# First two quarters of the first round's w2 in finished buffers, with 4 KB of scratch for dynamic transfers

## The reference

```python
def hier_moe(h, w_group, b_group, w_expert, b_expert, w1, w3, w2):
    ...                      # the router picks 2 of 64 experts for each token
    def expert_block(args):
        xb, e = args
        return (jax.nn.silu(xb @ w1[e]) * (xb @ w3[e])) @ w2[e]
    y_disp = lax.map(expert_block, (x_disp.reshape(n_blocks, MOE_BLOCK, d), blk_expert)).reshape(rows, d)
    y = jax.ops.segment_sum(y_disp[dest] * w_sorted[:, None].astype(y_disp.dtype), tok_sorted, num_segments=t)
    return y.reshape(b, s, d)
```

## Time and profile before

| | us |
|---|---|
| median of 3 runs | 1448.33 |
| lowest and highest | 1446.87, 1449.07 |
| the profiled execution's own time | 1447.13 |
| its span | 1445.3 |

### The profile page before, as it was taken

One profiled execution on the slowest core, in us unless ns is written; L12 is line 12 of the kernel. 1 busy time (PEld: TensorE's weight loads), 2 busy tenths in 40 slices (PEclk: granted clock), 3 DMA queues, 4 the chain that ended last, 5 costly groups with the idle time before them and its releaser, 6 DMA issues.

```text
span 1445.3 us, 14719 instructions
## 1 busy us (share of the span) xinstructions
PE 1028.2 (71%) x5933; PEld 532.5 (37%) x5933; DVE 457.4 (32%) x932; ACT 166.1 (11%) x409; POOL 59.1 (4%) x94
## 2 busy tenths in 40 slices
PE   4999999999999986466465664665645646566366
PEld 1867688655455442122121221212212212122121
DVE  1255477443467361121120211212112112021121
ACT  1132222012233210000000000000000000000000
POOL 4000210011020000000000000000000000000000
PEclk9999999999999999788887887878868878788688
DMA  9946656656626579999999999999999999999996
GB/s 352 370 169 239 240 219 233 230 95 204 225 85 243 205 296 428 428 428 428 427 429 428 429 428 428 429 429 428 429 429 429 429 429 428 429 429 427 428 426 260
DMA packets 78638, 503.75 MB, mean 349 GB/s; under 512 B 5318, under 2 KB 10718, under 8 KB 54020
## 3 DMA queue, kind: packets, MB, share of 16 engines
q1 hardware_dynamic: 75872, 496.22, 83.8%
q0 software_dynamic: 2656, 6.93, 2.1%
q10 hardware_dynamic: 68, 0.02, 0.0%
HBM read 501.54 MB, written 1.61 MB: 348 GB/s over the span
## 4 chain that ended last, share of the span: by engine, by line
PE 50%; DMA 41%; DVE 4%; SPq 3%; issue 1%; ACT 0%; DVEq 0%
DMA flex<-in_w_dram 23%; DMA arena<-in_w_dram 14%; PE ps L542 11%; PE ps L531 10%; PE ps L1011 9%; PE ps L1036 7%; PE ps L986 3%; PE ps L1054 2%; DMA ring<-in_w_in_dram 2%; DMA ring<-in_w_ada_dram 2%; SPq L387 1%; PE ps L768 1%; SPq L393 1%; DVE arena L2009 1%; PE ps L663 1%
## 5 line engine op out<-in xcount | busy, mean ns | idle before, releaser
L1011 PE MATMUL ps<-ring,arena 128*32 128x512 f32 x1024 | 258.8, 663 | 97.2 <-DMA arena<-in_w_dram 94.6
L1011 PE MATMUL ps<-arena 128*32 128x512 f32 x768 | 258.3, 662 | 96.7 <-DMA flex<-in_w_dram 93.9
L1036 PE MATMUL ps<-arena 128*32 128x512 f32 x384 | 146.6, 733 | 67.0 <-DMA flex<-in_w_dram 66.3
L1036 PE MATMUL ps<-ring,arena 128*32 128x512 f32 x512 | 146.7, 736 | 65.4 <-DMA arena<-in_w_dram 64.6
L542 PE MATMUL ps<-ring,flex 128*128 128x512 f32 (+1 forms) x368 | 155.7, 579 | 0.4 <-ACT flex L1104 0.4
L531 PE MATMUL ps<-flex,ring 128*128 128x256 f32 x640 | 147.7, 388 | 3.1 <-DMA ring<-in_w_in_dram 2.4
L1011 PEld LDWEIGHTS ps<-ring,arena 128*32 128x32 f32 x1024 | 66.5, 121 | 176.1 <-issue 174.7
L531 PEld LDWEIGHTS ps<-flex,ring 128*128 128x128 f32 x640 | 122.1, 194 | 22.1 <-issue 3.0
L1011 PE MATMUL ps<-flex,arena 128*32 128x512 f32 x256 | 129.6, 665 | 0.0
L1011 PEld LDWEIGHTS ps<-arena 128*32 128x32 f32 x768 | 60.2, 120 | 176.4 <-issue 173.6
L2009 DVE TENSOR_TENSOR arena<-ps,grow 128x1024 f32<-128x1024 f32 x15 | 18.4, 1224 | 264.3 <-PE ps L1036 264.3
(11 more groups left out here) (385 smaller groups left out, 1022.8 us busy)
## 6 DMA issues: line engine op xcount, KB each, us to landing
ring<-in_w_dram SPq DMA_DIRECT2D x92, 2048.0 KB, 19.8
arena<-in_w_dram SPq DMA_DIRECT2D x69, 2048.0 KB, 24.0
flex<-in_w_dram SPq DMA_DIRECT2D x23, 2048.0 KB, 28.6
ring<-in_w_in_dram SPq DMA_DIRECT2D x17, 2048.0 KB, 10.2
ring<-in_w_ada_dram SPq DMA_DIRECT2D x14, 2048.0 KB, 8.3
ring<-in_w_ada_dram SPq DMA_DIRECT2D x8, 1024.0 KB, 17.9
ring<-in_w_out_dram SPq DMA_DIRECT2D x4, 2048.0 KB, 9.7
ring<-in_w_dram SPq DMA_DIRECT2D x16, 512.0 KB, 13.2
```

What stands on the lines that cost most here:

```text
L1011: mm = pe.matmul(ps[32 * e:32 * e + 32, g, :], xe3[:, c, 32 * e:32 * e + 32], mslot(slots[e])[:, c * W5:(c + 1) * W5], start=c == 0, stop= ...
L1036: mm = pe.matmul(ps[32 * e:32 * e + 32, 2 + n, :], actT3[:, j, 32 * e:32 * e + 32], mslot(slots[e])[:, o:o + W5], start=j == 0, stop=j == ...
```

## The change

- **Pieces ahead.** Quarters 0 and 1 of round 0's w2 are cut in 16 pieces of 256 KB (quarter j, expert e, half n), each with a home outside the eight places: parts of `grow`, `arena`, `hoT`, `cst`, `wr`, `wrs`, `mod2p` whose contents are no longer needed, and six pieces in a new tensor `spare` (`ahead_of`). SP issues 12 of them behind the first load of w3, after waits for `st_wr` and `cv_w2`, and 4 behind the last load of w3, after waits for `x_ok` and `gr_sum`.
- **Quarters 2 and 3** of that w2 go into the first two quarters of places 0 to 3, at `first_free` 1 and 2.
- **w1 of round 1** is loaded in quarters too, at `second_free` 1 to 3 (raised at c = 1, 3, 5 of round 0's w3 product) and `mring_free` 2, where before it was four loads of 2 MB at `mring_free` 2. PE waits for the first three quarters on `third_in`.
- **Memory.** `hoT` is now declared with all 128 partitions (33 were used, and still are by its first reader). `spare` takes 12 KB of each partition, and the scratch that GpSimd's dynamic DMAs use shrinks from 16 KB to 4 KB of each partition.

```diff
+AHEAD = 2
...
-        hoT = sb("hoT", BM, parts=33)
+        hoT_all = sb("hoT", BM)
+        hoT = hoT_all[0:33, :]
+        spare = sb("spare", 6 * W5)
...
+        def ahead_of(j, e, n):
+            homes = [grow[:, 0:W5], grow[:, W5:D], ar(3584, W5), hoT_all[:, 0:W5], cst[:, C_S1:C_S1 + W5], wr[:, 0:W5]]
+            homes += [spare[:, k * W5:(k + 1) * W5] for k in range(6)]
+            homes += [grow[:, D:D + W5], grow[:, D + W5:2 * D], wrs[:, 0:W5], mod2p[:]]
+            return homes[8 * j + 2 * e + n]
...
-            def load_quarter(half, e, expert, j, signal):
+            def load_quarter(half, e, expert, j, signal, place=None):
                 q = group_of(half, 2)[0][e]
+                o = (j if place is None else place) * D
...
+            def load_ahead(k0, k1):
+                for k in range(k0, k1):
+                    j, e, n = k // 8, k % 8 // 2, k % 2
+                    src = w2[e:e + 1].rearrange("o (p r) n -> p r (o n)", p=P)[:, j, n * W5:(n + 1) * W5]
+                    sp.dma_start(ahead_of(j, e, n), src).then_inc(first_in[j], 16)
...
                     load(0, g, e, e)
+                    if g == 1 and e == 0:
+                        sp.wait_ge(st_wr, 16)
+                        sp.wait_ge(cv_w2, 2)
+                        load_ahead(0, 12)
+            sp.wait_ge(x_ok, 8)
+            sp.wait_ge(gr_sum, 1)
+            load_ahead(12, 8 * AHEAD)
+            for j in range(AHEAD, 4):
+                sp.wait_ge(first_free, j - AHEAD + 1)
+                for e in range(ITEMS):
+                    load_quarter(0, e, e, j, first_in[j] if j < 3 else None, j - AHEAD)
             for j in range(4):
                 if j < 3:
-                    sp.wait_ge(first_free, j + 1)
+                    sp.wait_ge(second_free, j + 1)
                 else:
-                    sp.wait_ge(mring_free, 1)
+                    sp.wait_ge(mring_free, 2)
                 for e in range(ITEMS):
-                    load_quarter(0, e, e, j, first_in[j] if j < 3 else None)
-            for n in range(3, 2 * GROUPS):
+                    q = group_of(1, 0)[0][e]
+                    src = w1[ITEMS + e:ITEMS + e + 1].rearrange("o (p r) n -> p (o r n)", p=P)[:, j * D:(j + 1) * D]
+                    sp.dma_start(mslot(q)[:, j * D:(j + 1) * D], src).then_inc(third_in if j < 3 else mring_in[q], 16)
+            for n in range(4, 2 * GROUPS):
...
+                    if second and g == 0:
+                        pe.wait_ge(third_in, 3 * 16 * ITEMS)
...
-                        if first and g == 0 and c in (1, 3, 5):
-                            mm.then_inc(first_free, 1)
+                        if first and c in (1, 3, 5):
+                            mm.then_inc((first_free, second_free)[g], 1)
...
-                    if j < 3 and (first or last):
+                    if first and j < AHEAD:
+                        pe.wait_ge(first_in[j], 16 * 2 * ITEMS)
+                    elif j < 3 and (first or last):
...
-                            o = j * D + n * W5
+                            o = (j - AHEAD if first else j) * D + n * W5
+                            w = ahead_of(j, e, n) if first and j < AHEAD else mslot(slots[e])[:, o:o + W5]
...
-    nc = _bacc.Bacc("TRN2", target_bir_lowering=False, num_devices=1)
+    nc = _bacc.Bacc("TRN2", target_bir_lowering=False, num_devices=1, dynamic_dma_scratch_size=4096)
```

More of the change, by code:

```diff
@@ L219, in build @@
         last_in = [sem(f"last_in{j}") for j in range(3)]
+        second_free, third_in = sem("second_free"), sem("third_in")
         first_free, t_y, t_ye = sem("first_free"), sem("t_y"), sem("t_ye")
@@ L387, in load @@
                 sp.dma_start(mslot(q), src).then_inc(mring_in[q], 16)
-            def load_quarter(half, e, expert, j, signal):
+            def load_quarter(half, e, expert, j, signal, place=None):
                 q = group_of(half, 2)[0][e]
+                o = (j if place is None else place) * D
                 src = w2[expert:expert + 1].rearrange("o (p r) n -> p r (o n)", p=P)[:, j, :]
-                sp.dma_start(mslot(q)[:, j * D:(j + 1) * D], src).then_inc(signal if j < 3 else mring_in[q], 16)
+                sp.dma_start(mslot(q)[:, o:o + D], src).then_inc(signal if j < 3 else mring_in[q], 16)
+            def load_ahead(k0, k1):
[3 more added lines that the diff above has]
+                    sp.dma_start(ahead_of(j, e, n), src).then_inc(first_in[j], 16)
             out_of_arena = [(att_ok, 2), (cp_p, 1)]
@@ L977, in block_experts, with round_ @@
                           stop=True).then_inc(r_it, 1)
-            def round_(k, half, first=False, last=False):
+            def round_(k, half, first=False, last=False, second=False):
                 it = k * 2 + half
@@ L1034, in round_ @@
                         for e in range(ITEMS):
-                            o = j * D + n * W5
-                            mm = pe.matmul(ps[32 * e:32 * e + 32, 2 + n, :], actT3[:, j, 32 * e:32 * e + 32],
-                                           mslot(slots[e])[:, o:o + W5], start=j == 0, stop=j == 3,
-                                           skip_group_check=True)
+                            o = (j - AHEAD if first else j) * D + n * W5
+                            w = ahead_of(j, e, n) if first and j < AHEAD else mslot(slots[e])[:, o:o + W5]
+                            mm = pe.matmul(ps[32 * e:32 * e + 32, 2 + n, :], actT3[:, j, 32 * e:32 * e + 32], w,
+                                           start=j == 0, stop=j == 3, skip_group_check=True)
                         if last and j == 3 and n == 0:
@@ L1061, in _ @@
             for half in range(2):
-                round_(0, half, half == 0)
+                round_(0, half, half == 0, second=half == 1)
             with pe.Fori(1, PAIRS - 1) as k:
@@ L2073, in _ @@
             pool.dma_start(rbx[0:32, :], t["rel_bias_2"]).then_inc(ld_rows1, 16)
-            pool.dma_start(hoT[:], t["buckets"]).then_inc(ld_rows1, 16)
+            pool.dma_start(hoT, t["buckets"]).then_inc(ld_rows1, 16)
             def below_diagonal(tile):
```

## The result

| | before | after |
|---|---|---|
| median us (runs) | 1447.60 (4) | 1438.88 (4) |
| lowest and highest | 1446.23, 1449.07 | 1438.02, 1441.07 |
| the profiled execution, its span | 1447.13, 1445.3 | 1441.07, 1439.3 |

The ratio of the runs is 0.994, with a 95% interval of 0.9927 to 0.9953: the kernel is 8.7 us faster. The forecast was 1438.9. The profiled execution after is the slowest of its four, and the two traces lie only 6.06 us apart, not 8.7.

The account below looks back on a forecast made before the run. Weight transfers bound the kernel from about 525 us: stream start plus bytes by rate plus a tail. Moving half of w2 gains 10.2, w1's quarters cost 0.8: 9.4 us off the median 1448.33 gives 1438.9, range 1436.5 to 1442.5.

Parts of the forecast that it names:

- What bounds: From about 525 us on, weight transfers at 426 to 429 GB/s bound the kernel; PE waits for them.
- Part 1, the 12 pieces: 3.15 million bytes at 397 GB/s, 7.9 us, fit the idle 483 to 498 us, with 7 us to spare.
- Part 2, the 4 pieces: 1.05 million bytes, 2.6 us at 397 GB/s, fit the idle 520 to 525 us, with 2 us to spare.
- Part 3, the sum: Half of round 0's w2 leaves the dense stream, 10.2 us; w1 by quarters costs 0.8; 9.4 us gained.
- Part 4, the feed: Transfers stay fed around 535 us with under 1 us to spare; nothing booked, up to 1 us in the range.
- PE in round 1: Features ready at 559.9 us against w1's data at 559.0: PE later by 0.9 us, which matters to nobody.
- Part 5, the scratch: Smaller scratch for POOL's dynamic transfers costs zero, as POOL's transfers have much time, 23 us of cover for wrs.
- The feed gap: Rival: stream starves around 535 us, pieces spill over 525, or PE's clock is low; price 1.5 to 6 us, chance 0.09.
- Small transfers: Rival: each of the 16 pieces costs a full latency, 4.4 us; 38 us slower, 1486; chance 0.02.
- a full ring: Rival: POOL's early loads go out in portions, PE stands 68 us from 44.8; 1507 us; chance 0.03.

## Why the prediction was right, point by point

- **What bounds.** Right. From the first quarter on, each kernel's end follows from bytes, rate and feed, but for up to 1 us at the very end. The long window reads 428 GB/s before and after.
- **Part 1, the 12 pieces.** Right: 398 GB/s for the pieces, as good as over by 493 (4 GB/s in the window from 493 to 494), ahead of SP's next issue at 498.98. The 397 that it took for them was read from a window that mixes rows of 2 KB and of 4 KB, so its fit is partly luck. It missed that six of SP's issues would take 12.85 us, which cost nothing on that queue.
- **Part 2, the 4 pieces.** Right in outcome. Together with the end of `flex` they moved between 519 and 525 at 333 GB/s and less, not at 397, and of the 2 us to spare 1 was left (16 GB/s in the window from 525 to 526, none from 526 to 527).
- **Part 3, the sum.** The price of w1's quarters was forecast at 0.8 and is 0.86. The bytes were forecast at 10.2. With the ends of the streams set equal, the first quarter brings 4.8 of its 5.1, and the second 903.97 - 899.84 = 4.1, and 0.7 and 0.6 more that the change lost at its dip and at its end (413 against 384 and 297 against 272 GB/s): 5.4. Together that is the 10.2.
- **Part 4, the feed.** Booked at nothing, with up to 1 us in the range. The dip cost 0.65. The step that was too kind is the time from issue to first bytes: "at least 0.65 us" was used, while full rate came more than 2 us after an issue into an empty queue.
- **What was not in the sum.** At its end the stream of the change lost (303 - 272) / 428 x 10 = 0.7 us against the kernel before, and no part of the prediction had a term for it. In all: 10.2 - 0.86 - 0.65 - 0.7 = 8.0, and the stream shrank by 8.0. The forecast of 9.4 was 1.4 us too high, and the median came out at 8.7 with a scatter of that size. The last landing was to be at 1422.8 and is at 1425.91: these 1.4 and the 1.7 of the dense part. That 1438.9 was hit to the decimal is luck.
- **PE in round 1.** Wrong in a detail that changed nothing. PE was to be 0.9 us later than w1's data of round 1. But they landed at 561.97 (543.87 + 18.10), and PE had stood for them, as its row in the timeline after says in brackets:

```profile
562.33 0.59 PE L1046 MATMUL ps<-arena 128*32 128x512 f32 x1 [1.81 <-DMA flex<-in_w_dram]
```

- **Part 5, the scratch.** The cost of zero is right, the reason was half right. "POOL's rows stand where they stood" is wrong: POOL stood for 8 us at one place, which no engine waited for. The cover that I had checked was another one, that of wrs.
- **The rivals.** The feed gap came, at less than half of its lowest price. Small transfers did not pay one by one. With the smaller scratch POOL did stand, at 13.5 and 22.6 us, and too briefly to reach PE; that a full ring is what held it is likely, but no row names it. No kernel with 4 KB hung. The Trainium skill, "DMA: Bandwidth & Descriptors", section "Bandwidth", gives 341 GB/s for a transfer of 1 MB, measured on transfers that GpSimd issues. Here pieces of 256 KB, queued by SP, ran at 398 GB/s, above it.

## What to carry to other kernels

Where transfers run without a pause to the end, find the idle stretches ahead of that, count them in bytes, and look for memory whose contents are finished; each million bytes put there was worth 2.2 to 2.3 us here, ahead of what it cost elsewhere (0.86 for w1 in quarters, 0.65 at the dip). Then look at what must be issued when the shortened part is over: without w1 in smaller loads, nearly a third of the gain (2.3 of 8.0 us) would have gone back into a hole of 4 us. And compare such kernels from a common event to the last landing, as the part ahead of it scattered by 5 us, and look at the last 10 us on their own, which scattered by 1 us here.

## What the runs showed of the hardware that was not expected

- With 4 KB of scratch rather than 16 KB for dynamic transfers, GpSimd stood 1.1 to 2.0 us ahead of its 19th transfer and 7.7 to 8.3 us ahead of its 21st, in every kernel that had it, and issued the latter at 22.5 to 22.9 us; with 16 KB it went at 13.2 to 13.4. No engine waited for it.
- Into an empty queue, transfers took 2 to 3 us from the issue to their full rate: 135 and 184 GB/s in the windows of 525 and 526, 401 in the next, for an issue at 524.35.
- SP's issue, 0.33 to 0.5 us as a rule, took up to 4.2 us for one piece with about ten transfers under way (472 to 485), and 14.3 us for one load at 32.35 with only three; the transfers went on meanwhile, at 409 GB/s in the first case and 406 from 22 to 46. So their number alone does not make it.
- In the last 10 us ahead of the last landing the rate was 267 to 311 GB/s, by the kernel, and not over 400 as ahead of that.
